# Two perceptrons on one Trainium2 core: the activations' sums laid elsewhere, and the squared rectifier of chunks 4 to 15 on ScalarE in two instructions

## What is computed

```
def squared_relu_mlp(h, w1, w2):
    return jnp.square(jax.nn.relu(h @ w1)) @ w2

        x = x + g2 * squared_relu_mlp(modulate(rms_norm(x, norm_mlp[i]), sh2, sc2), mlp_w1[i], mlp_w2[i])
        if not last:
            ctx = ctx + cg2 * squared_relu_mlp(modulate(rms_norm(ctx, norm_mlp[i]), csh2, csc2),
                                               mlp_w1[i], mlp_w2[i])
```

## Time and profile before

| what | value |
|---|---|
| median of 3 runs | 3803.15 us (3800.34 to 3805.57) |
| the profiled execution | 3803.46 us |
| its span in the trace | 3801.6 us |
| TensorE busy | 3682.5 us, 97% |
| VectorE busy | 2586.5 us, 68% |
| ScalarE busy | 1438.4 us, 38% |
| GpSimd busy | 328.6 us, 9% |
| mean granted clock of TensorE | 0.994 of full speed |

### The profile page before, as it was taken

How to read it: one execution, slowest core, us unless ns; L and a number is a source line. 1 busy time by engine, 2 the same in 40 slices (tenths; PEclk the granted TensorE clock), 3 DMA queues, 4 the chain that set the end, 5 groups by cost and what they waited for, 6 DMA issues and landing times. The chain is left out here.

```text
span 3801.6 us, 52485 instructions
## 1 busy us (share of the span) xinstructions
PE 3682.5 (97%) x19210; PEld 3102.1 (82%) x19210; DVE 2586.5 (68%) x4522; ACT 1438.4 (38%) x2574; POOL 328.6 (9%) x460
## 2 busy tenths in 40 slices
PE   8999999999999999999999999999999999999999
PEld 6888777888888877888877899888999868687887
DVE  6767674767766767567666378377777674647987
ACT  4223354222422234532224467333222454534432
POOL 0000021000000001200000011101112100001221
PEclk9999999999999999999999999999999999999999
DMA  6443312443444322134422121111112110002232
GB/s 249 134 132 100 111 34 96 145 132 119 145 134 133 115 71 74 67 121 136 133 75 77 49 58 44 38 68 56 67 67 70 65 47 1 28 29 83 95 107 82
DMA packets 96048, 341.38 MB, mean 90 GB/s; under 512 B 10815, under 2 KB 13247, under 8 KB 95068
## 3 DMA queue, kind: packets, MB, share of 16 engines
q1 hardware_dynamic: 73728, 264.96, 20.8%
q0 software_dynamic: 17152, 63.66, 5.2%
q10 hardware_dynamic: 4956, 9.90, 0.7%
HBM read 335.64 MB, written 7.39 MB: 90 GB/s over the span
## 5 line engine op out<-in xcount | busy, mean ns | idle before, releaser
L268 PE MATMUL ps<-h_hi,w_hi 128*128 128x512 f32 (+1 forms) x2194 | 861.0, 392 | 14.2 <-DVE w_lo L223 7.9
L269 PE MATMUL ps<-h_lo,w_hi 128*128 128x512 f32 (+1 forms) x2194 | 850.1, 387 | 0.0
L270 PE MATMUL ps<-h_hi,w_lo 128*128 128x512 f32 (+1 forms) x2194 | 849.8, 387 | 0.0
L223 DVE TENSOR_TENSOR w_lo<-w_first_raw,w_hi 128x1024 fp32r<-128x1024 f32 x243 | 297.2, 1224 | 311.7 <-ACT w_hi L208 311.5
L208 ACT ACTIVATE w_hi<-w_first_raw 128x1024 fp32r<-128x1024 f32 x241 | 254.8, 1058 | 652.1 <-PE ps L270 645.1
L268 PEld LDWEIGHTS ps<-h_hi,w_hi 128*128 128x128 f32 x2194 | 413.2, 188 | 107.0 <-DVE w_lo L223 12.5
L269 PEld LDWEIGHTS ps<-h_lo,w_hi 128*128 128x128 f32 x2194 | 413.4, 188 | 84.5 <-issue 3.4
L270 PEld LDWEIGHTS ps<-h_hi,w_lo 128*128 128x128 f32 x2194 | 413.0, 188 | 84.8
L268 PE MATMUL ps<-a_hi,w_hi 128*128 128x512 f32 x752 | 292.7, 389 | 6.7 <-DVE x L863 6.7
L269 PE MATMUL ps<-a_lo,w_hi 128*128 128x512 f32 x752 | 291.1, 387 | 0.0
L270 PE MATMUL ps<-a_hi,w_lo 128*128 128x512 f32 x752 | 291.0, 387 | 0.0
(11 more groups left out here) (369 smaller groups left out, 7154.8 us busy)
## 6 DMA issues: line engine op xcount, KB each, us to landing
w_first_raw<-in_w_first SPq DMA_DIRECT2D x213, 512.0 KB, 3.4
w_raw<-in_w_first SPq DMA_DIRECT2D x105, 512.0 KB, 3.4
shared<-in_w_ada POOLq DMA_DIRECT2D x96, 512.0 KB, 4.6
w_first_raw<-in_w_mlp SPq DMA_DIRECT2D x64, 512.0 KB, 3.5
w_raw<-in_w_mlp SPq DMA_DIRECT2D x64, 512.0 KB, 4.2
w_first_raw<-in_w_even SPq DMA_DIRECT2D x16, 512.0 KB, 3.5
near_stage<-in_near POOLq DMA_DIRECT2D x32, 256.0 KB, 2.9
w_first_raw<-in_w_odd SPq DMA_DIRECT2D x16, 512.0 KB, 3.5
```

The lines of the kernel that those rows point to most:

```text
L223: dve.tensor_tensor(lo, self.raw(n), hi.bitcast(F32), ALU.subtract).then_inc(self.lo_done, 1)
L268: pe.matmul(out, lhs[0], rhs[0], start=start, stop=False)
L269: pe.matmul(out, lhs[0], rhs[1], start=False, stop=False)
L270: return pe.matmul(out, lhs[1], rhs[0], start=False, stop=stop)
```

## The change

Three things change, all in the class `Perceptron`.

1. In chunks 4 to 15 the VectorE instruction `square(j)` is gone. ScalarE makes a Relu of `mid[:, j, :]` in place, waits for it on a new semaphore `bent`, makes a Square in place, and only then `high`. This is recorded ahead of `high(c, 0)` and ahead of `high(c, 1)`.
2. The ten fold steps are put in another order (the two that only finish buffer b come last), and are laid at other places among VectorE's work of chunks 0 to 3.
3. `fold_high` and `fold_low` of the sums 0 to 2 move with them.

The number of matmuls, loads and GpSimd instructions is the same, and so is the order on TensorE, GpSimd and SyncE.

```diff
-                         (b, b, q(1, 1, 1), ALU.add), (b, b, q(0, 1, 0), ALU.subtract),
-                         (b, b, q(1, 1, 0), ALU.subtract), (a, q(0, 1, 1), q(0, 0, 1), ALU.subtract),
-                         (a, a, q(1, 1, 1), ALU.add), (a, a, q(1, 0, 1), ALU.subtract))
+                         (b, b, q(1, 1, 1), ALU.add), (a, q(0, 1, 1), q(0, 0, 1), ALU.subtract),
+                         (a, a, q(1, 1, 1), ALU.add), (a, a, q(1, 0, 1), ALU.subtract),
+                         (b, b, q(0, 1, 0), ALU.subtract), (b, b, q(1, 1, 0), ALU.subtract))
...
             def fold_high(self, act, t):
-                act.wait_ge(self.folded, (3, 5, 10, 10)[t])
+                act.wait_ge(self.folded, (3, 5, 8, 10)[t])
...
             def scalar(self, act):
+                def square(c, j):
+                    act.wait_ge(self.combined, 4 * (c - self.plain) + 2 * j + 2)
+                    act.activation(mid[:, j, :], mid[:, j, :], ACT.Relu).then_inc(self.bent, 1)
+                    act.wait_ge(self.bent, 2 * (c - self.plain) + j + 1)
+                    act.activation(mid[:, j, :], mid[:, j, :], ACT.Square).then_inc(self.val_done, 1)
...
                             high(c, j)
-                            if c == 1:
-                                self.fold_high(act, j)
-                            if c == 3 and j == 0:
-                                self.fold_high(act, 2)
+                            if (c, j) in ((1, 1), (2, 0), (3, 0)):
+                                self.fold_high(act, c - 1)
...
                     keep(6, 1, 0, 0)
+                    square(c, 0)
                     high(c, 0)
+                    square(c, 1)
                     high(c, 1)
...
             def vector(self, dve):
-                            if c == 1:
-                                self.fold_steps(dve, (0, 3)[j], (3, 5)[j])
-                            if c == 2 and j == 0:
-                                self.fold_low(dve, 1)
-                                self.fold_steps(dve, 5, 6)
-                            if c == 3 and j == 0:
-                                self.fold_steps(dve, 8, 10)
+                            if j == 0 and c:
+                                self.fold_steps(dve, *((0, 2), (4, 6), (9, 10))[c - 1])
...
-                            if c == 2 and j == 0:
-                                self.fold_steps(dve, 6, 7)
-                        if c == 3:
-                            self.fold_low(dve, 2)
+                            if j == 0 and c in (1, 2):
+                                self.fold_steps(dve, *((2, 3), (6, 7))[c - 1])
+                            if j == 0 and c > 1:
+                                self.fold_low(dve, c - 1)
...
-                    square(0, 2)
                     combine(4, 6, 0, m11, m10, m11, ALU.add)
                     rest(c, 0)
                     combine(4, 7, 3, m10, m10, ps[:, 3, 0:half], ALU.subtract)
-                    square(1, 4)
...
-                        if c == 0 and o == 4:
+                        if c == 0 and o == 3:
+                            self.fold_steps(dve, 3, 4)
+                        if c == 0 and o == 6:
                             self.fold_low(dve, 0)
-                        if c == 1 and o == 4:
-                            self.fold_steps(dve, 7, 8)
+                        if c == 1 and o in (3, 6):
+                            self.fold_steps(dve, 7 + o // 6, 8 + o // 6)
```

More of the change, by code:

```diff
@@ L2796, in __init__ @@
                 self.val_done, self.hi_done, self.lo_done, self.x_done = S("val"), S("a_hi"), S("a_lo"), S("x_done")
+                self.bent = S("relu")
             def ready(self, pe, n):
@@ L2870, in fold_steps @@
                         dve.wait_ge(self.scaled[0], self.scaled[1])
-                    if n == 5:
-                        dve.wait_ge(self.t_lo, 2)
+                    if n in (5, 8):
+                        dve.wait_ge(self.t_lo, 1 if n == 5 else 2)
                     if n:
@@ L3118, in combine @@
                         dve.tensor_tensor(out, in0, in1, op).then_inc(self.combined, 1)
[L3120 to L3123, removed]
                     m00, m01, m10, m11 = (mid[:, j, a:a + half] for j in range(2) for a in (0, half))
```

## The result

| | median | range | runs |
|---|---|---|---|
| before | 3803.64 us | 3800.34 to 3812.36 | 6 |
| after | 3820.03 us | 3816.06 to 3824.31 | 6 |

The ratio after to before is 1.0040, 95% interval 1.0027 to 1.0054: 0.4% slower (the medians are 16.4 us apart), near the forecast's 3818. The profiled execution took 3820.92 us with a span of 3819.1, 17.5 longer than before, at the same mean clock of 0.994.

What follows compares the result with a forecast made beforehand. TensorE was taken as the bound, waiting only where VectorE lags by two outputs (first perceptron) or four (second). Terms +19.8 + 2.5 - 1.7 - 5.8 = +14.8 on 3803.46 gave 3818 us; 8-in-10 range 3806 to 3826.

Steps and rivals of the forecast that it cites:

- First perceptron: down(3) to down(13), timed from stage start D: ScalarE's squares make outputs 3 and 4 late, 1.8 us a stage, +19.8.
- the last pair: Last two down stages: +2.5 in the first perceptron; +1.2 for down(14) of the second, from ScalarE's longer chain.
- The step that I called the one that decides: First perceptron, VectorE: `rest` of half 0 waits 1.8 us for ScalarE and holds back the fourth `combine`.
- The squares on VectorE: First perceptron: removing two VectorE instructions of 0.96 a chunk is no gain, since TensorE does not wait there.
- Fold steps: First perceptron's down(0) -2.4 and down(2) -0.9, second's down(0) -2.5; together -5.8, ends 0 and -10.7.
- the mis-sized term: Second perceptron, nine stages: some 0.4 of the 0.65 wait at output 6 comes back in each, -3.6.
- GpSimd's third instruction ends at about D+1.6: Second perceptron: ends some 0.3 earlier than before, counted from stage start D; `rest` ends 0.55 behind it, D+2.1.
- what comes back without the meeting: Second perceptron: with no VectorE-GpSimd port lock, `rest` would end at D+1.7 and the whole 0.65 come back.
- down(3): Second perceptron: ScalarE's longer chain shows where nothing was lost before, +0.7.
- shorter waits: Rival: first perceptron waits only 1.3 a stage, second gives back all; +4.6, 3808 us; chance 0.15.
- faster: Rival: first perceptron does not wait at all, leaving -3.6 and -5.8; 3794 us; chance 0.06.
- slower still: Rival: second perceptron's `rest` waits for GpSimd's fourth instruction, nine stages lose 0.9 each; +11.7, 3830 us; chance 0.08.

Runs made afterwards that it cites:

- experiment 3: The changed kernel with VectorE's `rest` of half 0 moved behind the fourth `combine`; 3795.43 us, ratio 0.9979 to the kernel before.
- experiment 4: The changed kernel with ScalarE's first two high parts of the next weights ahead of its second Relu and Square; 3788.58 us, ratio 0.9961 to the kernel before.
- Experiment 10: The changed kernel with half 1's Relu on ScalarE done twice; 3840.39 us, ratio 1.0095 to the kernel before.
- Experiment 7: The kernel before with the new fold order and two high parts of next weights ahead of ScalarE's second activation high part, squares on VectorE; 3789.79 us, ratio 0.9968.
- experiment 1: The kernel before with the fold steps' new order alone, squares still on VectorE; 3799.33 us, ratio 0.9984.
- experiment 9: The changed kernel with GpSimd's four additions cut from 512 to 8 columns in chunks 5 to 15 of both perceptrons; 3815.73 us, ratio 1.0033 to the kernel before.
- experiment 2: The kernel before with the squares of chunks 4 to 15 on ScalarE, fold steps in their old places; 3831.49 us, ratio 1.0074.
- experiment 11: The kernel of weights' two high parts ahead of ScalarE's second Relu, with half 1's Relu done twice; 3800.35 us, ratio 0.9995 to the kernel before.
- Experiment 6: The changed kernel with half 0's square back on VectorE, half 1's still on ScalarE; 3800.86 us, ratio 0.9995 to the kernel before.

## Why the prediction came out

**First perceptron: right, step by step.** The high part of half 0 ended at D+1.11 as worked out; `rest` started at D+1.13 (forecast 1.14), the fourth `combine` at 2.01 (2.02), the second Relu at 2.59 (2.61), the weights' high part at 5.10 (5.12), their low part at 5.75 (5.77). The waits were 1.25 and 0.51 (1.26 and 0.43), a stage 18.66 on the mean (18.6), +20.5 for +19.8, and the last pair +2.6 for +2.5. Experiments 3 and 4 show that the steps were also the cause: taking either link out of the chain leaves ScalarE's work and removes most or all of the loss. Experiment 10 shows the chain of half 1 on the path for its whole length. The step that I called the one that decides, `rest` ahead of the fourth `combine`, is one of two: without the weights behind half 1 it costs nothing.

**The squares on VectorE were no load.** Experiment 7 shows it from the other side. The Trainium skill's rule, use VectorE and not ScalarE for relu and mul ("ScalarE: Activation LUTs", "Rules for kernel authors"), pointed the right way here, but by the price of an instruction. What experiments 4 and 7 show is that the two homes cost the same when nothing that TensorE needs stands behind them.

**Fold steps: right.** Forecast -2.4, -0.9 and -2.5; measured -2.25, -0.88 and -2.53, and the same three alone in experiment 1. The waits that were to stay did so: in the first down(0) outputs 3 and 4 are 1.4 and 1.0 late, and in down(2) output 7 waits 1.49 as before.

**Second perceptron: the mis-sized term.** Nine stages were to give -0.4 each, -3.6; down(4) to down(13) gave -1.6. The nine gave -2.2, and the tenth, down(11), which the sum left as it was, took 0.6 more. The step that failed is "GpSimd's third instruction ends at about D+1.6": in eight of the stages it ended at D+1.56 to D+2.12, on the mean at D+1.77. It moves with the landing of the load that starts GpSimd. Two stages of the kernel after, GpSimd's second and third addition:

```profile
3572.53 1.56 POOL L2891 TENSOR_TENSOR w_raw<-w_raw 128x512 f32<-128x512 f32 x1
3574.16 1.29 POOL L2893 TENSOR_TENSOR scratch<-w_raw 128x512 f32<-128x512 f32 x1
...
3593.92 1.30 POOL L2891 TENSOR_TENSOR w_raw<-w_raw 128x512 f32<-128x512 f32 x1
3595.30 1.35 POOL L2893 TENSOR_TENSOR scratch<-w_raw 128x512 f32<-128x512 f32 x1
```

The first is for the stage at 3573.33, where the third addition starts at D+0.83, and takes 11.69; the second for that at 3595.09, at D+0.21, and takes 11.12. Six lie between (D+0.28 to D+0.49, 11.20 to 11.44).

SP issues the two loads of a chunk 7.3 and 6.9 to 7.0 ahead of the stage in every one of the ten, and in these eight GpSimd starts, when the second has landed, 2.18 to 2.54 ahead. In down(11), at 3723.20, the load landed 2 later still, GpSimd met the low part of weights in place of `rest`, and the stage took 11.60; the one such before took 10.98. In down(13), at 3766.27, it landed 0.8 later, `rest` came before the third addition and took 0.69, and the stage took 10.91: there a later load was luck. Why the landing differs from stage to stage was not tried. With the same order in these stages experiment 2 has 114.4, so the -1.6 of one execution is itself good to about 1.

The sentence of the prediction on what comes back without the meeting (`rest` at D+1.7, the whole 0.65) is what experiment 9 measured. It gives the rule on the port of the Trainium skill ("SBUF — State Buffer", "SBUF: two separate sides") a second witness: 0.69 instead of 1.31 for VectorE's low part, with GpSimd's additions the only thing cut.

down(3) took +0.3 (+0.7 forecast), but not by ScalarE's longer chain, as the prediction has it: GpSimd starts 2.47 ahead of it (0.54 before), `rest` takes 1.17, and with GpSimd cut short the stage takes 10.91. The last pair took +1.3 (+1.2), in experiment 9 as well.

By the stages the change costs 17.5 where the sum said 14.8: 2.0 of the difference is this term, 0.7 the eleven stages.

**Rivals.** None of the three came ("shorter waits", "faster", "slower still"). The last had its mechanism in part: a late `rest` does stretch a stage, but in the changed kernel it met the third addition and not the fourth.

## What to carry to other kernels

Before work is moved to an engine with time to spare, write down what stands behind it in that engine's queue and who waits for that: here 3.4 us more work in each chunk of the first perceptron, for a ScalarE that is busy 40% of the span, cost 1.87 a stage because the next weights stood behind it, and another order (experiment 4) made it free. The gap that such a wait opens is the place for the work that it holds up. A wait of 1.9 us in a trace is no cost in itself; follow it to the engine that sets the time, and take out each link of the chain by itself.

## What was not expected of the hardware

- The stages repeat to 0.1 us, the times do not. In the profiled execution of experiment 11 the first down stage started at 2520.01, in that of experiment 4 at 2503.69, before anything that the edits touch. The granted clock of two stretches ahead of the perceptrons differs, first before, then in experiment 11:

```profile
400.00:800.00 400.00, 384.85 (x1896) 0.99 0.28 94
1200.00:1600.00 400.00, 383.97 (x1886) 0.99 0.26 85
```

```profile
400.00:800.00 400.00, 385.25 (x1854) 0.96 0.27 91
1200.00:1600.00 400.00, 384.12 (x1869) 0.97 0.24 79
```

  Cut finer, again first before, then in experiment 11:

```profile
400.00:410.00 10.00, 7.84 (x43) 1.00 0.48 159
410.00:420.00 10.00, 10.00 (x40) 0.83 0.15 52
420.00:430.00 10.00, 10.00 (x42) 1.00 0.01 2
```

```profile
400.00:410.00 10.00, 7.84 (x41) 0.95 0.48 159
410.00:420.00 10.00, 10.00 (x28) 0.50 0.17 52
420.00:430.00 10.00, 10.00 (x26) 0.53 0.00 0
```

  In both the clock falls behind 10 us in which TensorE is busy for 7.84. In experiment 11 it then stays at the lower of the two levels (0.50, 1.2 GHz) for most of 20 us, though TensorE is busy throughout; in the kernel before it is at 1.00 again in the third stretch. Why it stays down longer in one execution is open. Experiment 6, whose first down stage started at 2517.87, shows 0.97 in both long stretches, experiments 1 and 3 in the second. So a difference of a few us is better read from the stages than from two times.
- Expected, and so it was: Relu and Square took what a copy of the same shape takes, 0.85 for 128x768, and the Square that waits for the Relu ahead of it on ScalarE started 0.03 after its end (2646.45 + 0.85, 2647.33).
